# Three pairs of weight tiles moved by 32, 64 and 96 bytes in SBUF

## The chip, the cores and the metric

The kernel runs on one core of one Trainium2 chip. The metric is the device time of one execution in microseconds (us). Before the change the median of three runs is 2806.64 us (2805.08 to 2807.08).

## The reference, cut to what matters

Two small transformer stacks are run one after the other on one sequence of 256 tokens with 2048 features, all in float32. The first has two layers: a mixer (a recurrent and a gated-delta branch in the even layer, three kinds of sparse attention in the odd one) and a gated feed-forward block of inner width 5632. The second has two layers of attention variants with narrower projections. Nearly all of the arithmetic is in products of this kind:

```python
z = (u @ w_in).astype(jnp.float32)            # 256 x 2048 by 2048 x up to 8208
gate, up = jnp.split(u @ w_gu, 2, axis=-1)    # 256 x 2048 by 2048 x 11264
return (jax.nn.silu(gate) * up) @ w_down      # 256 x 5632 by 5632 x 2048
return o.astype(u.dtype) @ w_out
```

Every weight is used once per execution, and 481 MB are moved by DMA in all.

## The kernel before, in words

**The products.** A float32 matrix product is made of three products in the faster format fp32r. The activations are split into a high and a low part (`UTH`, `UTL` for the input of a stage; `HTH`, `HTL` for the hidden layer of the feed-forward block), and so are the weights (`WH`, `WL`). The kernel adds high by high, high by low and low by high. The activation tile of 128 x 128 is TensorE's stationary operand (LDWEIGHTS), and 512 columns of a weight tile are the moving operand. Lines 1105 to 1107 do this in `col` (input projections and the first feed-forward product), lines 1152 to 1154 in `row` (output projections and the second feed-forward product).

**The weights.** They come in slots of 512 KB, 1024 float32 elements on each of 128 partitions. The SP queue loads a slot into one of four `RAW` tiles. ScalarE copies it rounded to fp32r into `WH` (line 1628), VectorE writes the difference of `RAW` and `WH` to `WL` (line 2150), and TensorE then does 12 matmuls with it. A pair `WH`, `WL` is called a home. Three homes are allocated on their own (`NW = 3`) and take turns for most slots; each is used again three slots later. Six further homes (`XH`, `XL`) lie over parts of the tiles `WORK` and `BIG` and are used only for some slots at the end of each stage and the start of the next, when those parts are free.

**Two other kinds of matmul that the prediction reads.** The step `nar` (lines 1121 and 1122) handles two narrow groups of weight columns: there the weight tile in a home is the stationary operand (32 or 96 columns of it), and `UTH` or `UTL` is the moving one, with 256 columns. The step `hg_e` (lines 1354 and 1355) multiplies stationary tiles in `ZR`, which lies over `BIG`, with moving columns of the constant tile `WC`, in fp32r too.

**The order.** The order in which the steps are issued on each engine is written out ahead of time by one function (`write_order`), and every engine follows it; semaphores hold an engine back until its operands are there. The change doesn't touch this order.

**Where the tiles lie.** Tiles are allocated one behind the other. The lengths of `UTH`, `UTL` (16,384 bytes each on a partition) and of every home tile (4,096 bytes) are multiples of 256, and so is that of `WORK`. So `UTH`, `UTL`, all `WH` and `WL`, `WORK` and the start of `BIG` have one and the same remainder by 256. `HTH`, `HTL`, `XH` and `XL` are placed over `WORK` and `BIG` at multiples of 256 bytes and have it too. `BIG` is 65,664 bytes long, which is 128 more than a multiple of 256, so that `RAW`, `H`, `WC` and what follows stand 128 bytes off. The second half of `ZR` (tokens 128 to 255) begins 32,832 bytes behind its first, which puts it 64 bytes off.

Of the kernel before, what the change touches and what calls it, by code (L numbers as in the profile page):

```python
# [8 lines left out]
F32R = mybir.dt.float32r  # L9
# [7 lines left out]
SLOT = 1024  # L17
NRAW = 4
NW = 3
# [164 lines left out]
def v3(ap, a):  # L184
    return ap.rearrange("p (a b) -> p a b", a=a)
# [594 lines left out]
def build(nc, A, out):  # L780
    with ExitStack() as ctx:
        def sb(name, n, dt=F32):
            return ctx.enter_context(nc.sbuf_tensor(name, [128, n], dt))

        def over(name, n, at):

            return nc.alloc_sbuf_tensor_at(name, [128, n], dtype=F32R, offset=at)[:]
# [6 lines left out]

        UTH = sb("UTH", NKT * 256, F32R)[:].rearrange("p (k n) -> p k n", k=NKT)
        UTL = sb("UTL", NKT * 256, F32R)[:].rearrange("p (k n) -> p k n", k=NKT)
        WHL = [(sb(f"WH{i}", SLOT, F32R)[:], sb(f"WL{i}", SLOT, F32R)[:]) for i in range(NW)]
        work_at = -(-nc.sbuf_base // 32) * 32
        WORK = sb("WORK", 10752)[:]
        big_at = -(-nc.sbuf_base // 32) * 32  # L800
# [4 lines left out]
        room = [work_at + 4096 * i for i in range(8)] + [big_at + 4 * a for a in (5184, 6400, 7424, 15360)]  # L805
        WHL += [(over(f"XH{i}", SLOT, room[2 * i]), over(f"XL{i}", SLOT, room[2 * i + 1])) for i in range(NX)]
        WC = sb("WC", 9 * 128, F32R)[:]
# [190 lines left out]
        def slot_of(s):  # L998
            src, kk, wd = slots[s]
            n = kk * wd  # L1000
            wh, wl = WHL[home[s]]
            if wd < 64:
# [43 lines left out]
        def tensor(e):  # L1046
# [64 lines left out]
            def nar(st, c, k, s):  # L1111
                wd = WIDTHS[st][c]
                both = v3(WHL[home[s]][0][:, 0:16 * wd], 8)
                if k == 0:
# [1832 lines left out]
```

## Time and profile before

| what | value |
|---|---|
| median of three runs | 2806.64 us |
| the profiled execution, its own time | 2806.17 us |
| its span, first to last instruction | 2804.4 us |
| mean granted TensorE clock | 0.999 of full speed |
| TensorE (PE) busy | 2778.6 us, 99% of the span |
| VectorE (DVE) busy | 1577.9 us, 56% |
| ScalarE (ACT) busy | 1369.2 us, 49% |
| DMA | 481 MB, mean 172 GB/s |

Busy time is a union: matmuls overlap in the pipeline, so one matmul is listed with some 390 ns although the next one starts some 227 ns after it. For the rate of TensorE the distance between starts is read, not the duration. `PEld` is the loading of the stationary operand, which overlaps the matmul before it. The page is divided into 40 slices of 70 us, and PE is at 9 tenths or more in all but the last.

### The profile page before, as it was taken

Reading aid. Unit: us, or ns where it says so; the run is one execution under the profiler, and the core shown is the slowest. Engines: PE = TensorE matmul, PEld = TensorE weight load, DVE = VectorE, ACT = ScalarE, POOL = GpSimd, SP = SyncE. Lnnn points to the kernel's source line nnn. Section 1 sums busy time; section 2 is a strip of 40 time slices with the busy share of each in tenths; the row PEclk is TensorE's granted clock in tenths of the full one; section 3 lists DMA queues with packets and bytes.
Section 4 is the critical chain, followed back from the end, with each engine's and each line's share of the span. In section 5 each row is a group of like instructions: output and inputs, shape, how many; then the busy total and the mean of one; then the engine's idle time right before and its main releaser. Section 6 shows DMA issues by size and latency. Waiting matters only on the chain.

```text
span 2804.4 us, 33205 instructions
## 1 busy us (share of the span) xinstructions
PE 2778.6 (99%) x13548; PEld 2318.0 (83%) x13548; DVE 1577.9 (56%) x2212; ACT 1369.2 (49%) x2031; POOL 62.0 (2%) x83
## 2 busy tenths in 40 slices
PE   9999999999999999999999999999999999999998
PEld 8788888888888888888888888888888888887777
DVE  6665677755445454444644555654545544466666
ACT  6645454545444444333634544644444443356565
POOL 0000000000000000000010000000000000000002
PEclk9999999999999999999999999999999999999999
DMA  7855544665656555555655434566565555565444
GB/s 234 139 128 131 108 106 99 165 211 180 189 186 191 191 188 189 193 193 192 219 170 156 136 106 151 191 192 190 188 192 188 188 191 192 195 206 170 152 142 135
DMA packets 213497, 481.12 MB, mean 172 GB/s; under 512 B 15584, under 2 KB 16352, under 8 KB 212704
## 3 DMA queue, kind: packets, MB, share of 16 engines
q1 hardware_dynamic: 210848, 467.78, 55.0%
q0 software_dynamic: 2352, 11.17, 1.1%
q8 instruction: 106, 1.74, 0.3%
q14 instruction: 47, 0.39, 0.0%
q10 hardware_dynamic: 144, 0.05, 0.0%
HBM read 476.84 MB, written 2.10 MB: 171 GB/s over the span
## 4 chain that ended last, share of the span: by engine, by line
PE 90%; DVE 5%; ACT 2%; DMA 1%; issue 1%; POOL 0%; SPq 0%; ACTq 0%; POOLq 0%
PE PS L1105 19%; PE PS L1107 19%; PE PS L1106 18%; PE PS L1152 8%; PE PS L1154 8%; PE PS L1153 8%; DVE WL L2150 1%; DVE WORK L2309 1%; PE PS L1366 1%; ACT WH L1628 1%; PE PS L1269 1%; PE PS L1486 1%; PE PS L1184 1%; PE PS L1281 1%; PE PS L1282 1%
## 5 line engine op out<-in xcount | busy, mean ns | idle before, releaser
L2150 DVE TENSOR_TENSOR WL<-RAW,WH 128x1024 fp32r<-128x1024 f32 x826 | 1010.9, 1225 | 934.0 <-ACT WH L1628 932.6
L1628 ACT ACTIVATE WH<-RAW 128x1024 fp32r<-128x1024 f32 x830 | 875.1, 1055 | 833.9 <-PE PS L1107 526.3
L1105 PE MATMUL PS<-WH,UTH 128*128 128x512 f32 x2396 | 955.9, 399 | 3.4 <-DVE WL L2150 3.0
L1107 PE MATMUL PS<-WH,UTL 128*128 128x512 f32 x2396 | 935.0, 390 | 0.0
L1106 PE MATMUL PS<-WL,UTH 128*128 128x512 f32 x2396 | 933.8, 390 | 0.0
L1105 PEld LDWEIGHTS PS<-WH,UTH 128*128 128x128 f32 x2396 | 450.2, 188 | 98.8 <-issue 3.7
L1107 PEld LDWEIGHTS PS<-WH,UTL 128*128 128x128 f32 x2396 | 449.8, 188 | 97.2
L1106 PEld LDWEIGHTS PS<-WL,UTH 128*128 128x128 f32 x2396 | 450.6, 188 | 87.2
L1152 PE MATMUL PS<-WH,HTH 128*128 128x512 f32 x656 | 255.4, 389 | 0.0
L1153 PE MATMUL PS<-WL,HTH 128*128 128x512 f32 x656 | 255.2, 389 | 0.0
L1154 PE MATMUL PS<-WH,HTL 128*128 128x512 f32 x656 | 255.2, 389 | 0.0
L1153 PEld LDWEIGHTS PS<-WL,HTH 128*128 128x128 f32 x656 | 123.1, 188 | 25.7
L1152 PEld LDWEIGHTS PS<-WH,HTH 128*128 128x128 f32 x656 | 123.1, 188 | 25.4
L1154 PEld LDWEIGHTS PS<-WH,HTL 128*128 128x128 f32 x656 | 123.1, 188 | 25.4
L1152 PE MATMUL PS<-WH,UTH 128*128 128x512 f32 x256 | 102.1, 399 | 1.4 <-DVE UTL L2198 1.4
L1154 PE MATMUL PS<-WH,UTL 128*128 128x512 f32 x256 | 99.9, 390 | 0.0
L1153 PE MATMUL PS<-WL,UTH 128*128 128x512 f32 x256 | 99.7, 390 | 0.0
L2755 POOL TENSOR_TENSOR SM<-SM 128x1 f32<-128x1 f32 (+2 forms) x25 | 27.5, 1100 | 2347.6 <-DVE SM L2154 2347.6
L2150 DVE TENSOR_TENSOR XL<-RAW,XH 128x1024 fp32r<-128x1024 f32 x53 | 63.9, 1218 | 13.4 <-ACT XH L1628 13.3
L1659 ACT ACTIVATE UTH<-PS,GP 128x128 fp32r<-128x128 f32 x160 | 46.3, 387 | 40.4 <-PE PS L1080 40.4
L1628 ACT ACTIVATE XH<-RAW 128x1024 fp32r<-128x1024 f32 x53 | 55.3, 1066 | 19.4 <-DMA RAW<-in_ffn_w_down 7.8
L1752 ACT ACTIVATE HTH<-PS 128x512 fp32r<-128x512 f32 x44 | 26.1, 599 | 78.2 <-PE PS L1184 78.2
(421 smaller groups left out, 2412.5 us busy)
## 6 DMA issues: line engine op xcount, KB each, us to landing
RAW<-in_ffn_w_gu SPq DMA_DIRECT2D x352, 512.0 KB, 4.2
RAW<-in_ffn_w_down SPq DMA_DIRECT2D x176, 512.0 KB, 4.5
RAW<-in_ab_w_in SPq DMA_DIRECT2D x128, 512.0 KB, 4.7
RAW<-in_nsa_w_in SPq DMA_DIRECT2D x80, 512.0 KB, 3.6
RAW<-in_w_in SPq DMA_DIRECT2D x64, 512.0 KB, 4.0
RAW<-in_ab_w_out SPq DMA_DIRECT2D x32, 512.0 KB, 4.6
RAW<-in_nsa_w_out SPq DMA_DIRECT2D x32, 512.0 KB, 4.0
RAW<-in_w_out SPq DMA_DIRECT2D x16, 512.0 KB, 4.4
```

Source lines behind the costliest of these rows:

```text
L1105: e.matmul(o, lh, wh[:, j], start=k + j == 0, stop=False)
L1106: e.matmul(o, lh, wl[:, j], start=False, stop=False)
L1107: x = e.matmul(o, ll, wh[:, j], start=False, stop=k + j == NKT - 1)
L1152: e.matmul(o, lh, wh[:, 0, cs], start=k == (0 if hf else LEFT[st][0]), stop=False)
L1153: e.matmul(o, lh, wl[:, 0, cs], start=False, stop=False)
L1154: x = e.matmul(o, ll, wh[:, 0, cs], start=False, stop=k == (KTILES[st] - 1 if hf else LEFT[st][-1]))
L1184: x = e.transpose(b[:, 128 * j:128 * j + 128], g[:, 128 * j:128 * j + 128], ident)
L1269: x = e.matmul(b[:, 128 * h:128 * h + 128], LT[:, h], XX[:, h, 0], start=True, stop=True)
L1281: e.matmul(bb[:, 0:128], XX[:, h, 1], Y[:, h], start=True, stop=True)
L1628: e.activation(wh, raw, ACTF.Copy).then_inc(*a_hi.inc(s))
L1659: e.activation(UTH[:, kk, 128 * t:128 * t + 128], b[:, 128 * j:128 * j + 128], ACTF.Copy, scale=GP[:, st, kk:kk + 1]).then_inc(*a_ut.inc(" ...
L2150: e.tensor_tensor(wl, raw, wh.bitcast(F32), ALU.subtract).then_inc(*v_lo.inc(s))
```

## The change

Unused gaps of 8 float32 elements (32 bytes on each partition) are allocated in front of each of the three homes. They add up: the first home stands 32 bytes off its former remainder, the second 64, the third 96. A last gap of 160 bytes behind the third home brings the sum to 256, so that `WORK`, `BIG`, `RAW` and everything behind them move by 256 bytes and keep their remainders. The six homes over `WORK` and `BIG` keep theirs as well. No instruction is added, removed or reordered; only addresses differ.

```diff
-        WHL = [(sb(f"WH{i}", SLOT, F32R)[:], sb(f"WL{i}", SLOT, F32R)[:]) for i in range(NW)]
+        WHL = []
+        for i in range(NW):
+            sb(f"GAP{i}", 8)
+            WHL.append((sb(f"WH{i}", SLOT, F32R)[:], sb(f"WL{i}", SLOT, F32R)[:]))
+        sb("GAP", 40)
```

## Rows read from the trace of the kernel before

**Rows 1.** The page, part 1: busy time, share of the span and instructions of each engine.
```profile
PE 2778.6 (99%) x13548; PEld 2318.0 (83%) x13548; DVE 1577.9 (56%) x2212; ACT 1369.2 (49%) x2031; POOL 62.0 (2%) x83
```
**Rows 2.** The page, part 4: the chain that ended last, by engine, by line.
```profile
PE 90%; DVE 5%; ACT 2%; DMA 1%; issue 1%; POOL 0%; SPq 0%; ACTq 0%; POOLq 0%
PE PS L1105 19%; PE PS L1107 19%; PE PS L1106 18%; PE PS L1152 8%; PE PS L1154 8%; PE PS L1153 8%; DVE WL L2150 1%; DVE WORK L2309 1%; PE PS L1366 1%; ACT WH L1628 1%; PE PS L1269 1%; PE PS L1486 1%; PE PS L1184 1%; PE PS L1281 1%; PE PS L1282 1%
```
**Rows 3.** Waits of PE: who waited for whom, total us, times, longest us.
```profile
PE PS L1105 <- DVE WL L2150: 3.0, 6, 0.7
PE PS L1354 <- DVE ZR L2427: 1.7, 1, 1.7
```
**Rows 4.** Windows, first feed-forward block: stretch, length, busy by engine, PEclk, DMA.
```profile
620.00:1350.00 730.00, 730.00 (x3277) 603.78 (x3276) 368.75 (x360) 318.82 (x370) 2.36 (x4) 1.00 0.59 190
```
**Rows 5.** PE groups by form: count | busy us, mean ns | idle before.
```profile
L1105 PE MATMUL PS<-WH,UTH 128*128 128x512 f32 x2396 | 955.9, 399 | 3.4 <-DVE WL L2150 3.0 <-DVE WL L2167 0.2
L1152 PE MATMUL PS<-WH,HTH 128*128 128x512 f32 x656 | 255.4, 389 | 0.0
L1152 PE MATMUL PS<-WH,UTH 128*128 128x512 f32 x256 | 102.1, 399 | 1.4 <-DVE UTL L2198 1.4
```
**Rows 6.** PE timeline: start us, us, what; undisturbed stretch of the down product.
```profile
1199.69 0.39 PE L1153 MATMUL PS<-WL,HTH 128*128 128x512 f32 x1
...
1227.34 0.39 PE L1152 MATMUL PS<-WH,HTH 128*128 128x512 f32 x1
```
**Rows 7.** Line 1105: duration ns min/median/max of loads and matmuls.
```profile
L1105 PEld LDWEIGHTS PS<-WH,UTH x2396: 186/188/192, 9.4 to 2768.8; 128*128 128x128 f32 x200
L1105 PE MATMUL PS<-WH,UTH x2396: 387/389/582, 9.4 to 2769.0; 128*128 128x512 f32 x200
```
**Rows 8.** PE timeline, the narrow step: home as stationary operand.
```profile
84.33 0.28 PE L1122 MATMUL PS<-UTL,WH 128*32 128x256 f32 x1
...
87.80 0.28 PE L1122 MATMUL PS<-UTL,WH 128*32 128x256 f32 x1
```
**Rows 9.** Line 1121: duration ns min/median/max of its loads.
```profile
L1121 PEld LDWEIGHTS PS<-UTH,WH x32: 107/135/165, 84.1 to 1428.4; 128*32 128x32 f32 x16, 128*96 128x96 f32 x16
```
**Rows 10.** PE timeline: moving tile WC, then the homes, no break between.
```profile
268.55 0.50 PE L1354 MATMUL PS<-WC,ZR 128*128 128x512 f32 x1 [1.69 <-DVE ZR L2427]
268.89 0.39 PE L1355 MATMUL PS<-WC,ZR 128*128 128x512 f32 x1
...
269.58 0.40 PE L1105 MATMUL PS<-WH,UTH 128*128 128x512 f32 x1
...
272.12 0.39 PE L1107 MATMUL PS<-WH,UTL 128*128 128x512 f32 x1
```
**Rows 11.** PE timeline: the homes after four transposes.
```profile
950.49 0.60 PE L1184 MATMUL PS<-MK,BIG 128*128 128x128 f32 x4
950.84 0.48 PE L1105 MATMUL PS<-WH,UTH 128*128 128x512 f32 x1
951.16 0.40 PE L1106 MATMUL PS<-WL,UTH 128*128 128x512 f32 x1
...
953.47 0.39 PE L1107 MATMUL PS<-WH,UTL 128*128 128x512 f32 x1
953.71 0.60 PE L1184 MATMUL PS<-MK,BIG 128*128 128x128 f32 x4
```
**Rows 12.** Lines 2150 and 1628: duration ns min/median/max, by home tile.
```profile
L2150 DVE TENSOR_TENSOR WL<-RAW,WH x826: 1204/1225/1821, 12.1 to 2783.6; 128x1024 fp32r<-128x1024 f32 x166
L2150 DVE TENSOR_TENSOR XL<-RAW,XH x53: 1207/1217/1227, 610.1 to 2785.9; 128x1024 fp32r<-128x1024 f32 x53
L1628 ACT ACTIVATE WH<-RAW x830: 293/1061/1102, 11.0 to 2782.5; 128x1024 fp32r<-128x1024 f32 x165, 128x384 fp32r<-128x384 f32 x1
```

## The prediction, written before the changed kernel was run

> **What bounds the kernel now.** I read the busy times first: PE is busy for 99% of the span, DVE for 56%, ACT for 49% [rows 1]. The reader is to see that one engine fills the time. The chain of waits agrees: 90% of it is PE, and the six lines of the weight products (1105 to 1107, 1152 to 1154) hold 80% by themselves; the first DVE entry, line 2150, has 1% [rows 2]. The waits of PE come next: the largest, on line 2150's `WL`, is 3.0 us in six waits [rows 3]. So neither the preparation of weights nor their loading sets the time; what counts is how fast TensorE takes one matmul after the other. In the feed-forward block PE is busy for all of 730 us at a granted clock of 1.00, the upper level of 2.4 GHz [rows 4].
>
> The last view is the timeline, for the distance between starts. From 1199.69 to 1227.34 us there are 122 steps from one start to the next with nothing in between, so one takes 27.65 / 122 = 226.6 ns [rows 6]. 512 columns at 2.4 GHz are 213.3 ns. **The excess is 13.3 ns per matmul**, and it is the only thing on the critical path that an address could touch. How many matmuls have a moving operand in one of the three homes that move? Three kinds by (2396 + 656 + 256) = 3 x 3308 = 9924 [rows 5]. The excess over them is 9924 x 13.3 ns = 132 us. One nanosecond per matmul is 9.9 us, 0.35% of the time.
>
> **The change part by part.**
>
> *Instructions.* The gaps issue none, and order, semaphores and DMAs are as before. Cost: 0.
>
> *ACT and DVE.* They write the homes at other addresses, and DVE reads them. The bound of what an address may do to them is taken from their own spread: line 2150 has 1204 to 1225 ns (minimum, median) in the homes and 1217 ns in the six others, and line 1628 has a median of 1061 ns [rows 12]. Say 20 ns either way for each of 826 slots. That is 16.5 us of an engine that is idle for 44% of the time. On the chain line 2150 has 1%, some 28 us [rows 2]; 2% of this is 0.6 us. PE's waits for it would move by six times 20 ns [rows 3]. I take 0 and keep 1 us either way. If TensorE became faster by the whole excess, 12 matmuls per slot would take 12 x 213 = 2.56 us against 1.23 us of DVE, so there is cover in that case too.
>
> *TensorE, the moving operand.* This is the whole question, and the trace has no matmul that reads at 32, 64 or 96 bytes off. I bound it by the rows.
>
> From below: the whole excess goes, -132 us. The nearest row to a smaller gain is the spread of line 1105: the shortest matmul lasts 387 ns against a median of 389 [rows 7]. 2 ns on each of 9924 is -20 us.
>
> What the excess depends on can be read in two places. In the narrow step 30 steps from start to start take 87.80 - 84.33 = 3.47 us, 115.7 ns each [rows 8]; 256 columns at 2.4 GHz are 106.7 ns, an excess of 9.0 ns. There the load of the next stationary tile is of 32 columns (107 ns, against 188 ns for 128 columns [rows 7, 9]), and the start of that tile moves by 128 bytes from one pair to the next. So with a quarter of the loaded columns, half of the moving columns and a stationary operand that alternates between two remainders, two thirds of the excess are still there. That speaks for a cost of starting and streaming a matmul rather than for one of two reads that meet in the same place in memory.
>
> The second place is `hg_e`. Its moving tile `WC` stands 128 bytes off, its stationary tile 0. Three steps from 268.89 to 269.58 us take 0.69 us, 230 ns each [rows 10]: not below 226.6. A relative remainder of 128 brings no gain. The sample is small and lies right behind a wait.
>
> From above: after an interruption the rate isn't at 226.6 at once. From 951.16 to 953.71 us there are 11 steps in 2.55 us, 231.8 ns each [rows 11]. I call this settling; it costs 11 x 5.2 = 57 ns. The same is seen with no interruption at all where the moving tile changes from `WC` to a home: from 269.58 to 272.12 us 11 steps take 2.54 us, 230.9 ns each, 47 ns in excess [rows 10]. If each change between homes had to settle anew, 826 times 57 ns would be +47 us. It is an upper end, since slots behind an interruption pay this already.
>
> A smaller upward term: the excess grows with the columns, from 9.0 ns at 256 to 13.3 ns at 512 [rows 6, 8]. An operand that starts in the middle of a piece needs one piece more. With 16 pieces of 32 columns, one more is 13.3 / 16 = 0.8 ns: 9924 x 0.8 = +8 us.
>
> I take 0 for this part. It is the value nearest to what both places show, and the ends -132 and +47 us stay for the range.
>
> The Trainium skill ("SBUF — State Buffer", section Specifications) gives lines of 16 bytes. By that rule, 32, 64 and 96 bytes are whole lines, every read begins at a line as before, and the sum stays 0; no row shows a line. It also says ("TensorE: Matmul & The Clock Gate", section Step-by-step: what each phase is for) that the load of the next weights has its own read port and takes nothing from the running matmul. By that the stationary and the moving tile can't meet, whatever their remainders, and the change does nothing. Rows 8 agree in part. The same page ("Back-to-back issue gap") has 512 / 2.4 + 2.5 = 215.8 ns for a warm matmul of 512 columns, 10.8 ns below this kernel's; if the homes' old remainder were the reason for the difference, an estimate from that page would be 9924 x 10.8 ns = 107 us of gain. The trace has no fp32r matmul at that rate.
>
> *The sum* is 0. It is made against the profiled execution: span 2804.4 us, and 1.8 us around it, 2806.17 us. The median of the runs is 2806.64 us, 0.5 us above. I predict 2806.5 us.
>
> **The rivals.**
>
> *Faster: the two reads of TensorE meet, and the new remainders part them.* For it: the excess is there in each matmul and too regular to come from other engines, and the settling after an interruption shows that the distance depends on how the load and the matmul stand to each other, which is what two readers in each other's way would show. Against it: rows 8 and 10. Its time runs from 2806 - 20 = 2786 us (2 ns per matmul) to 2806 - 132 = 2674 us. The homes differ, so that one offset may help and another not; I take the row's 2 ns to a third of the excess (44 us) as its usual size, 2762 to 2786 us.
>
> *Slower: each change of home unsettles the stream.* Today all homes have one remainder, and going from home to home costs nothing: in the 122 steps of rows 6 there are some ten such changes. With three remainders each change moves the moving operand against the stationary one by 32 bytes or more, as the step from `WC` to the homes does. It decides at each slot's first matmul, and costs at most 47 us, 2853 us; half of it, if the next remainder is near, gives 2830 us. Against it: rows 10 are one case, itself close behind a wait of 1.69 us, and the stationary tile changes there too.
>
> *Slower by a little: one piece more per read.* 2806 + 8 = 2814 us.
>
> *The change doesn't do what it says.* The allocator could round starts up to a coarser boundary and swallow the gaps. Then the time is 2806 us as in the main case.
>
> **How the numbers follow.** The forecast of no change, the swallowed gaps included, gets 0.39; its own range is 2802 to 2811 us. The faster rival gets 0.33, of which 0.12 is for a gain over 40 us. The unsettled stream gets 0.18 and the longer read 0.10. A change of under 0.2%, 5.6 us, can't be told from none here. So faster 0.33, same 0.39, slower 0.28. The range reaches down to 2766 us, which leaves out the deep gains (0.12), and up to 2842 us, which leaves out the full settling (0.06).
>
> **What would show it.** Right: the same 122 steps in 27.6 us in the down product, a median of 389 ns on lines 1105 and 1152, and unchanged waits of PE. Faster rival: starts closer than 226 ns in the undisturbed stretches, with a step between homes. Unsettled stream: distances of 224 to 236 ns that return at every twelfth matmul. Longer read: an even 227.4 ns. If starts are as before but DVE's or ACT's durations move by over 20 ns, I was wrong on those, and the time should still stand. The prediction as a whole is wrong if the distance in those stretches moves by over 0.6 ns either way.

## The result, and the profile after

The changed kernel takes 2848.98 us (median of four runs, 2848.07 to 2850.08) against 2806.06 us for the kernel before on the same chip (2805.08 to 2807.08). The ratio is 1.0151, 95% interval 1.0138 to 1.0163: **slower by 43 us, 1.5%**. The forecast was no change, 2806.5 us, with a range up to 2842 us; it was wrong, and the range too narrow. Some runs of every kernel in the first set of experiments, the kernel before included, had a mean granted clock of 0.997 instead of 0.999 and took 5 to 8 us longer, which widens the intervals given there.

The page, parts 1 and 4, of the changed kernel. All lines below 797 have moved down by 4, so line 1105 is 1109 here.

```profile
PE 2823.1 (99%) x13548; PEld 2318.8 (81%) x13548; DVE 1578.4 (55%) x2212; ACT 1368.1 (48%) x2031; POOL 61.7 (2%) x83
...
PE 92%; DVE 4%; ACT 2%; issue 1%; DMA 1%; POOL 0%; SPq 0%; ACTq 0%; POOLq 0%
```

PE is busy for 44.5 us more than in [rows 1], with the same number of instructions, and the other engines for as long as before to within 1.1 us. PE's share of the chain grew from 90% [rows 2] to 92%. The whole loss is on TensorE. Its largest wait, 3.0 us before [rows 3], hardly changed:

```profile
PE PS L1109 <- DVE WL L2154: 2.6, 6, 0.7
```

The median durations of VectorE's and ScalarE's work on the homes (line, counts, ns minimum/median/maximum, as in [rows 12]) are within 2 ns of before:

```profile
L2154 DVE TENSOR_TENSOR WL<-RAW,WH x826: 1206/1226/1639, 12.2 to 2826.4; 128x1024 fp32r<-128x1024 f32 x166
L1632 ACT ACTIVATE WH<-RAW x830: 294/1059/1101, 11.1 to 2825.3; 128x1024 fp32r<-128x1024 f32 x165, 128x384 fp32r<-128x384 f32 x1
```

The granted clock is 1.00 in the first feed-forward block, as in [rows 4]; the columns of this window are stretch, length, busy time by engine, PEclk, DMA share and GB/s. 3250 matmuls are in 740 us, 4.39 per us, where it was 3277 in 730 us, 4.49.

```profile
630.00:1370.00 740.00, 740.00 (x3250) 599.36 (x3249) 365.56 (x354) 314.75 (x364) 1.79 (x3) 1.00 0.61 185
```

Line 1109's matmul has a median of 395 ns against 389 [rows 7]; its load is unchanged at 188 ns:

```profile
L1109 PEld LDWEIGHTS PS<-WH,UTH x2396: 185/188/193, 9.4 to 2811.5; 128*128 128x128 f32 x200
L1109 PE MATMUL PS<-WH,UTH x2396: 387/395/587, 9.4 to 2811.7; 128*128 128x512 f32 x200
```

The timeline says where. These are the first matmuls of four slots in a row in the undisturbed down product, the second feed-forward product (start us, us, what), in the same product as [rows 6]. By the written order the first of them is in the second home (64 bytes off), then come the third (96), the first (32) and the second again.

```profile
1220.17 0.40 PE L1156 MATMUL PS<-WH,HTH 128*128 128x512 f32 x1
...
1222.93 0.40 PE L1156 MATMUL PS<-WH,HTH 128*128 128x512 f32 x1
...
1225.74 0.39 PE L1156 MATMUL PS<-WH,HTH 128*128 128x512 f32 x1
...
1228.54 0.40 PE L1156 MATMUL PS<-WH,HTH 128*128 128x512 f32 x1
```

A slot is 12 matmuls. It takes 2.76 us in the home at 64 bytes, 2.81 us in the one at 96 and 2.80 us in the one at 32: 230.0, 234.2 and 233.3 ns per matmul, where before it was 226.6 in all three. **Each home has a speed of its own.** I added up the distances from each of the 10,560 large matmuls to the next one where both are of that kind: 2372.4 us before, 2417.6 us after, +45.2 us. That is the whole of the 43 us, within 2 us. In the home at 64 bytes the first distance of a slot is 237 to 241 ns and the others are 225 to 232 ns; in the home at 96 bytes they run from 231 to 240 ns to the slot's end.

### The profile page after: what moved, and what is told of

The parts are those of the page before. It is cut to its first block, busy times and chain, and to the rows that moved or that the text cites. A ratio compares the mean times of both kernels' runs of the same rounds, so it can differ in the third digit from the quotient of the medians.

```text
span 2847.1 us, 33205 instructions
## 1 busy us (share of the span) xinstructions
PE 2823.1 (99%) x13548; PEld 2318.8 (81%) x13548; DVE 1578.4 (55%) x2212; ACT 1368.1 (48%) x2031; POOL 61.7 (2%) x83
## 4 chain that ended last, share of the span: by engine, by line
PE 92%; DVE 4%; ACT 2%; issue 1%; DMA 1%; POOL 0%; SPq 0%; ACTq 0%; POOLq 0%
PE PS L1109 19%; PE PS L1110 19%; PE PS L1111 19%; PE PS L1156 8%; PE PS L1158 8%; PE PS L1157 8%; DVE WL L2154 1%; PE PS L1370 1%; DVE WORK L2313 1%; PE PS L1273 1%; PE PS L1490 1%; PE PS L1188 1%; ACT WH L1632 1%; PE PS L1285 1%; PE PS L1286 1%
## 5 line engine op out<-in xcount | busy, mean ns | idle before, releaser
L1111 PE MATMUL PS<-WH,UTL 128*128 128x512 f32 x2396 | 945.4, 395 | 0.0
L1110 PE MATMUL PS<-WL,UTH 128*128 128x512 f32 x2396 | 945.4, 395 | 0.0
L1158 PE MATMUL PS<-WH,UTL 128*128 128x512 f32 x256 | 101.1, 395 | 0.0
L1157 PE MATMUL PS<-WL,UTH 128*128 128x512 f32 x256 | 100.9, 394 | 0.0
```

Of the source, the lines that this page charges most:

```text
L1110: e.matmul(o, lh, wl[:, j], start=False, stop=False)
L1111: x = e.matmul(o, ll, wh[:, j], start=False, stop=k + j == NKT - 1)
L1157: e.matmul(o, lh, wl[:, 0, cs], start=False, stop=False)
L1158: x = e.matmul(o, ll, wh[:, 0, cs], start=False, stop=k == (KTILES[st] - 1 if hf else LEFT[st][-1]))
```

## The experiments

Unless a diff says otherwise, gaps are put so that everything but the named tiles keeps its remainder. "At 32" means 32 bytes off the old common remainder. The diffs are shortened to the lines that matter, and `k` counts the tiles of 128 rows of the weight matrix, 44 in the down product.

**all32, all64, all96: one remainder for all homes.** Two of my theories fit a sum of 43 us. Either each home's own remainder has a price, or it is the change from one remainder to the next that has one. The forecast's slower rival was the second, and its price, up to 47 us, hit the sum well.

```diff
-            sb(f"GAP{i}", 8)
+            if i == 0: sb("GAP0", 8)     # 16 in all64, 24 in all96
...
-        sb("GAP", 40)
+        sb("GAP", 56)                    # 48 in all64, 40 in all96
```

> All three homes stand 32 bytes off, with no change of remainder from home to home. Level theory (the distance between starts is set by the remainder of the moving tile against the stationary one, home by home): 233.2 ns per matmul in the undisturbed stretches, as the first home shows in the changed kernel, so 9924 x (233.2 - 226.7) = +65 us, 2871 us. Settling theory (it is the change from one home's remainder to the next that costs): 226.7 ns and about 2807 us, apart from the few changes to the six other homes.

> All three homes 64 bytes off. Level theory: 229.0 ns, the level that the second home reaches in the changed kernel, +23 us, 2829 us. Settling theory: 226.7 ns and about 2807 us.

> All three homes 96 bytes off. The third home of the changed kernel has a mean of 234.1 ns but no steady distance within its 12 matmuls. Level theory: about 234 ns, +73 us, 2879 us; if that home was still settling when it ended, its steady distance may lie lower, down to 230 ns, 2840 us. Settling theory: 226.7 ns and about 2807 us.

Measured: all32 2856.75 us, ratio 1.0168 (1.0150 to 1.0186); all64 2821.42 us, 1.0043 (1.0027 to 1.0059); all96 2858.93 us, 1.0174 (1.0157 to 1.0190). The timelines of the down product, first row and last of four slots, 48 distances; all32, then all64, then all96:

```profile
1223.49 0.40 PE L1157 MATMUL PS<-WH,HTH 128*128 128x512 f32 x1
...
1234.69 0.40 PE L1157 MATMUL PS<-WH,HTH 128*128 128x512 f32 x1
```

```profile
1208.40 0.39 PE L1157 MATMUL PS<-WH,HTH 128*128 128x512 f32 x1
...
1219.39 0.39 PE L1157 MATMUL PS<-WH,HTH 128*128 128x512 f32 x1
```

```profile
1225.20 0.39 PE L1157 MATMUL PS<-WH,HTH 128*128 128x512 f32 x1
...
1236.40 0.39 PE L1157 MATMUL PS<-WH,HTH 128*128 128x512 f32 x1
```

11.20, 10.99 and 11.20 us over 48 are 233.3, 229.0 (228.9 before the starts are rounded) and 233.3 ns, though no home differs from the next. The settling theory wanted 226.7 in all three and falls. The level theory holds. Its times were too high by 14, 8 and 20 us: I had multiplied the difference by all 9924 matmuls, but in stretches that are often interrupted the kernel before has 228.5 ns already, so there the loss is smaller (all32 has 233.1 there). For all96 the level was also 0.8 ns lower than assumed. The mean of the three times is 2845.7 us. The changed kernel has a third of each and takes 2849.0 us, so **some 3 us of the 43 are left for changing from home to home**. This difference of 3.3 us is no wider than the intervals of the runs that it is made of, some 4 us each way, and they stand on two chips. The traces show that it isn't nothing: in the down product the changed kernel's mean distance is 232.5 ns against 231.8 for the mean of the three levels, and on all matmuls in the homes those 0.65 ns would be 6 us. It is a small part either way.

**ut64: is it the tile's place or its place against the stationary one?**

```diff
+        sb("GAPU", 16)                   # UTH, UTL, WH, WL at 64
         UTH = sb("UTH", NKT * 256, F32R)[:]...
...
+        sb("GAP", 48)                    # behind the homes
```

> UTH, UTL and the three homes all stand 64 bytes off the old remainder; HTH and HTL keep it. So in the input projections and the attention output projections the moving and the stationary tile agree again, and in the down product they differ by 64 bytes. If the remainder of the moving tile against the stationary one counts: 226.7 ns in the projections, 229.0 ns in the down product, 1968 x 2.3 ns = +5 us, 2811 us. If the moving tile's own remainder counts: 229.0 ns in both, 2829 us. Settling theory: 226.7 ns in both, 2807 us.

Measured: 2812.50 us, ratio 1.0018 (1.0006 to 1.0029), the 2811 us of the first theory within its interval. The timeline, 48 distances each: the gate and up product, where both tiles stand at 64, and the down product, where only the homes do.

```profile
667.43 0.39 PE L1112 MATMUL PS<-WL,UTH 128*128 128x512 f32 x1
...
678.31 0.39 PE L1112 MATMUL PS<-WL,UTH 128*128 128x512 f32 x1
...
1203.60 0.39 PE L1158 MATMUL PS<-WH,HTH 128*128 128x512 f32 x1
...
1214.58 0.39 PE L1158 MATMUL PS<-WH,HTH 128*128 128x512 f32 x1
```

10.88 us are 226.7 ns, and 10.98 us are 228.8 ns (228.9 before rounding, the level of all64). Where the tiles were moved together nothing was lost. The six homes over `WORK` and `BIG` kept their place, so that in the projections they stand 64 bytes below `UTH` and `UTL`: their mean distance rose from 229.1 to 233.5 ns (interruptions left out) though they weren't moved. **What counts is the moving tile's remainder against the stationary one's.**

**utl32: one of the two stationary tiles.**

```diff
+        sb("GAPU", 8)
         UTL = sb("UTL", NKT * 256, F32R)[:]...
+        sb("GAP", 56)
```

> Only UTL stands 32 bytes off; UTH, HTH, HTL and all homes keep the old remainder. While the matmul of line 1105 streams WH, UTH is loaded for line 1106; while line 1106 streams WL, UTL is loaded for line 1107; while line 1107 streams WH, UTH is loaded for the next. If the moving tile meets the tile that is loaded meanwhile, one distance of three changes, after line 1106, by up to 6.7 ns and by at most 2.2 ns on average in the projections: 2596 x 6.7 = up to +17 us, 2825 us, and 226.7 ns stay in the down product. If it is the matmul's own stationary tile, the distance after line 1107 changes instead. If the moving tile's own remainder counts, nothing changes: 2807 us.

Measured: 2844.27 us, ratio 1.0135 (1.0119 to 1.0150). No theory had that. First the gate and up product, then the down product, 48 distances each:

```profile
673.50 0.40 PE L1112 MATMUL PS<-WL,UTH 128*128 128x512 f32 x1
...
684.70 0.40 PE L1112 MATMUL PS<-WL,UTH 128*128 128x512 f32 x1
...
1220.97 0.39 PE L1158 MATMUL PS<-WH,HTH 128*128 128x512 f32 x1
...
1231.85 0.39 PE L1158 MATMUL PS<-WH,HTH 128*128 128x512 f32 x1
```

The down product, which doesn't read `UTL`, stays at 226.7 ns. The other has 233.3 ns on average: the same price as if all pairs were 32 bytes apart, though only one of three is. By line:

```profile
675.36 0.40 PE L1111 MATMUL PS<-WH,UTH 128*128 128x512 f32 x1
675.60 0.40 PE L1112 MATMUL PS<-WL,UTH 128*128 128x512 f32 x1
675.84 0.39 PE L1113 MATMUL PS<-WH,UTL 128*128 128x512 f32 x1
676.06 0.40 PE L1111 MATMUL PS<-WH,UTH 128*128 128x512 f32 x1
```

On average over the gate and up products, the distance to the next start is 238.9 ns after the matmul that streams `WL`, during which `UTL` is loaded, 228.4 after the one that uses `UTL` and 232.4 after the third. The longest is where the moving tile and the tile being loaded meanwhile differ, as one theory said; but the others grew as well, so the price doesn't add up pair by pair. That a delay is carried into the next matmuls would explain it and isn't shown. It isn't shown either that the moving tile has to be one of the pair: in this run `UTL` also differs from `UTH`, the tile loaded before and after it. The loads last 188 ns as before.

**p128, p16, wlx: other remainders, and a search for a better one.** The first diff is p128's, the second p16's, the third wlx's, in which only the `WL` move.

```diff
-            sb(f"GAP{i}", 8)
+            sb(f"GAP{i}", (32, 8, 8)[i])             # at 128, 160, 192
...
-        sb("GAP", 40)
+        sb("GAP", 16)
```

```diff
+            at, n = homes_at + 8192 * i + off // 32 * 32, off % 32 // 4    # off is 16, 48, 224
+            WHL.append((over(f"WH{i}", SLOT + n, at)[:, n:], over(f"WL{i}", SLOT + n, at + 4096)[:, n:]))
```

```diff
+            at = homes_at + 8448 * i                 # off is 64, 128, 192
+            WHL.append((over(f"WH{i}", SLOT, at), over(f"WL{i}", SLOT, at + 4096 + off)))
```

> A probe of three more remainders: the homes stand 128, 160 and 192 bytes off. Relative-remainder theory: each home has a distance of its own again. The case of UTH 64 bytes above the six other homes (192 relative) had about 233 ns, so the third home should be near 233; a pattern that repeats every 128 bytes would give 226.7 ns for the first and 233 for the second, but would need 229 for the third. A pattern symmetric about 128 would give 229 for the third as well and is already in doubt. If 128 is free of it altogether, the first home has 216 to 226 ns and all homes at 128 would beat the kernel before.

> Three further remainders: 16, 48 and 224 bytes. If the levels come from a grid of 32 bytes or coarser, 16 behaves like 0 or 32 (226.7 or 233.3 ns) and 48 like 32 or 64 (233.3 or 229.0). If the start of a read inside a 32-byte unit costs a piece of its own, both lie above 233 ns. 224 tells whether a moving tile 32 bytes below the stationary one costs the same as one 32 above (233.3 ns) or not. A theory in which the remainder 0 is the best of all puts all three above 226.7.

> All WH keep the old remainder; WL stands 64, 128 and 192 bytes off in the three homes. A search for a layout better than the kernel before: one of three matmuls streams WL while UTL (or HTL) is loaded. utl32 had a distance of 233.3 ns with a single pair 32 bytes apart. If the common remainder is the best there is, all three homes have means above 226.7 ns (229 to 233). A home below 226.7 ns would be a layout to use: 1 ns is 10 us.

Measured: p128 2852.67 us, 1.0165 (1.0148 to 1.0182); p16 2846.06 us, 1.0140 (1.0125 to 1.0156); wlx, one run, 2839.66 us against 2806.08 us. A slot's length in the timeline is 12 distances of its home. In p128 this is a slot of the home at 128 bytes, its first matmul and that of the next slot:

```profile
1227.65 0.39 PE L1157 MATMUL PS<-WH,HTH 128*128 128x512 f32 x1
...
1230.43 0.39 PE L1157 MATMUL PS<-WH,HTH 128*128 128x512 f32 x1
```

2.78 us over 12 are 231.7 ns (231.6 in the mean of all such slots). All levels stand in this table; those of p128 and p16 are means of the distances in one home over the down products, which hold what is left from the home before:

| remainder, bytes | distance, ns | read from |
|---|---|---|
| 0 | 226.7 | rows 6, before rounding |
| 16 | 231.7 | p16 |
| 32 | 233.3 | all32 |
| 48 | 230.1 | p16 |
| 64 | 228.9 | all64 |
| 96 | 233.3 | all96 |
| 128 | 231.6 | p128 |
| 160 | 233.7 | p128 |
| 192 | 232.4 | p128 |
| 224 | 233.9 | p16 |

In wlx the three homes have means of 231.1, 233.2 and 230.0 ns with `WL` at 64, 128 and 192. A grid of 32 bytes is refuted (16 is neither 0 nor 32), and so is a repeat every 128. A piece of its own for a start inside a 32-byte unit asked for more than 233 ns at 16 and 48 bytes, and falls as well. 32 bytes below the stationary tile (224) cost 233.9 ns, nearly what 32 above do. Nothing is below the common remainder, and **no layout tried beats the kernel before**.

**m32at0, m32at32, m64at32: a smaller load.** If the reads of the load get in the way of the moving stream, fewer of them should cost less.

```diff
+                        m = 32 if st in (1, 3) and 0 < k < KTILES[st] - 1 else 128
-                        e.matmul(o, lh, wh[:, 0, cs], ...)
+                        e.matmul(o[0:m], lh[:, 0:m], wh[:, 0, cs], ...)    # the same for the other two
```

> Homes as before. In the down product all matmuls but the first and last k load only 32 of the 128 columns of the stationary tile, so the load lasts 107 ns instead of 188; three quarters of those output rows are left out (the output isn't the reference's). If the excess over 213.3 ns comes from the load's reads meeting the moving tile's, it shrinks with the load, to a quarter if it is proportional: 213.3 + 3.3 = 217 ns in the down product. If it belongs to the moving stream alone: 226.7 ns.

> As m32at0, with all homes 32 bytes off. If the load's reads meet the moving tile's, the 6.7 ns that 32 bytes cost shrink with the load, to some 1.7 ns: 218 to 219 ns. If the price of 32 bytes is that of a read that begins inside a piece, it stays at 6.7 ns above m32at0 whatever is loaded.

> As m32at32 with 64 columns loaded in place of 32. Load theory: between m32at32 and all32, near 213.3 + 20 / 2 = 223 ns. Moving-stream theory: 233.3 ns, as in all32.

Measured, one run each: 2815.91, 2855.49 and 2850.85 us against 2806.08 us. m32at0, 48 distances in the down product:

```profile
1134.82 0.40 PE L1154 MATMUL PS<-WL,HTH 128*32 128x512 f32 x1
...
1145.94 0.40 PE L1154 MATMUL PS<-WL,HTH 128*32 128x512 f32 x1
```

11.12 us are 231.7 ns: with a quarter of the load, 107 ns long, the distance at the common remainder *grew* by 5 ns. m32at32 has 233.3 ns (11.20 us) and m64at32 230.8 ns (11.08 us). The load theory had two halves, and they fared differently. The excess over 213.3 ns at the common remainder should have shrunk with the load; it grew, so that half is refuted. The *price of 32 bytes* should have shrunk from 6.7 ns to a quarter, 1.7 ns; it did: 11.20 - 11.12 = 0.08 us over 48 distances are 1.7 ns, where a price of the moving stream alone would have stayed at 6.7. One pair of runs can't say whether this is a proportion or a coincidence of two levels, and with 64 columns loaded the partner at the common remainder wasn't run. Fewer loaded columns are also fewer output rows, so these runs change both. That load and stream stand in each other's way by their timing fits all of this and is argued, not shown.

**n256at0, n256at32: 256 moving columns.** Each matmul of the down product is made as two; k 0 and the last are left whole.

```diff
+                        for a, z in ((0, 256), (256, 512)):
+                            cc = slice(512 * n + a, 512 * n + z)
+                            e.matmul(o[:, a:z], lh, wh[:, 0, cc], ...)    # the same for the other two
```

> Homes as before. In the down product each matmul of 512 columns is made as two of 256 for all but the first and last k. If the excess of 13.3 ns is paid per matmul (a handover): 106.7 + 13.3 = 120 ns each. If it belongs to the moving stream (a share of its columns): 106.7 + 6.7 = 113.3 ns each and no change of the time. The narrow step had 115.7 ns at 256 columns with 32 loaded.

> As n256at0 with all homes 32 bytes off. Handover theory: 106.7 + 20 = 126.7 ns each. Stream theory: 106.7 + 10 = 116.7 ns each.

Measured, one run each: 2833.27 and 2861.86 us against 2806.59 us. 96 distances of each, n256at0 first:

```profile
1131.46 0.28 PE L1156 MATMUL PS<-WH,HTH 128*128 128x256 f32 x1
...
1142.98 0.28 PE L1156 MATMUL PS<-WH,HTH 128*128 128x256 f32 x1
```

```profile
1150.17 0.28 PE L1161 MATMUL PS<-WH,HTH 128*128 128x256 f32 x1
...
1161.48 0.28 PE L1161 MATMUL PS<-WH,HTH 128*128 128x256 f32 x1
```

11.52 / 96 = 120.0 ns: at the common remainder the excess is 13.3 ns for 256 columns as for 512. This is what **a price per matmul** gives, 32 cycles of 2.4 GHz. But these runs also load 128 columns for every 256 moving ones, and the loads may set a part of the 120.0 ns. The kernel before has a case where little but the loads is left: eight float32 matmuls (not fp32r) of 15 moving columns, each with a load of 128:

```profile
1487.35 0.96 PE L1447 MATMUL PS<-WORK 128*128 128x15 f32 x8
```

From the second on they start 111 to 112 ns apart. So a floor of the loads near 112 ns is a rival for the last 8 ns, and no run here parts the two. At 32 bytes 11.31 / 96 = 117.8 ns: neither theory, and less than at 0. So 32 bytes are 6.7 ns worse at 512 columns and 2.2 ns better at 256. The kernel is slower all the same: its other products stay at 512, and two halves of 117.8 ns are longer than one whole of 226.7.

**bf16at0, bf16at32: 2 bytes per column.** For k 0 to 21 of the down product the same tiles are read as bfloat16 (the stationary view begins 2 bytes into its tile); the true sum then starts at k 22, so half of that product is left out.

```diff
+                        if st in (1, 3) and k < 22:
+                            cb = slice(1024 * n, 1024 * n + 512)
+                            lh, ll = lh.bitcast(BF)[:, 1::2], ll.bitcast(BF)[:, 1::2]
+                            e.matmul(o, lh, wh[:, 0].bitcast(BF)[:, cb], ...)    # and the other two
```

> Homes as before. In the down product the matmuls of k 0 to 21 read the same tiles as bfloat16 (512 moving columns of 2 bytes, 128 stationary columns at a step of 4 bytes); their sums are thrown away, so half of that product is left out. If the excess needs 4 bytes per moving column: 216 ns or less than 220, against 226.7 in k 22 to 43. If it doesn't: 226.7 ns.

> As bf16at0 with all homes 32 bytes off. If the sensitivity to the remainder comes from the 4 bytes per moving column, the distance in k 0 to 21 equals that of bf16at0 within 0.5 ns, against 233.3 ns in k 22 to 43. If not, 6 to 7 ns more than in bf16at0.

Measured, one run each: 2794.61 and 2838.05 us against 2806.59 us. bf16at0 first, then bf16at32; 49 distances each (of one matmul between them the record is missing):

```profile
1134.36 0.38 PE L1157 MATMUL PS<-WH,HTH 128*128 128x512 bf16 x1
...
1144.94 0.38 PE L1158 MATMUL PS<-WL,HTH 128*128 128x512 bf16 x1
```

```profile
1152.20 0.38 PE L1162 MATMUL PS<-WH,HTH 128*128 128x512 bf16 x1
...
1162.77 0.38 PE L1163 MATMUL PS<-WL,HTH 128*128 128x512 bf16 x1
```

10.58 us and 10.57 us: 215.9 and 215.7 ns, the same at both remainders. With bfloat16 32 bytes don't matter (no other remainder was tried) and four fifths of the excess are gone. Two things changed here at once, the width of the moving columns and the load, which lasts 98 ns in place of 188; the run doesn't say which of them frees it. The back-to-back distance in the Trainium skill ("TensorE: Matmul & The Clock Gate", Back-to-back issue gap), 215.8 ns at 512 columns, agrees with these rows and holds for no fp32r row here.

## Why the prediction was wrong

*The bound: right.* TensorE sets the time, the distance between starts is the quantity to read, there are 9924 matmuls concerned, and one nanosecond on each is 9.9 us. The sign named for being wrong, a distance that moves by over 0.6 ns, came: it moved by 3.4 to 7.6 ns. PE's busy time grew by 44.5 us and the time by 43.

*ACT, DVE and the waits: right.* Medians moved by 1 and 2 ns, the largest wait of PE from 3.0 to 2.6 us.

*TensorE's moving operand: the step that failed.* "I take 0 for this part" should have been +43 us, 4.3 ns on each of the 9924 matmuls on average. In the undisturbed stretch the distance went from 226.7 to 230.0, 234.2 and 233.3 ns. Two readings led to the 0.

The narrow step [rows 8] was read as evidence that the excess is a cost of starting and streaming, on which addresses have no hold. It has 256 moving columns and a short load, and n256at0, n256at32 and m32at0 show that both change how the remainder acts. A case that differs in three sizes can't stand in for the one in question. That the excess grows with the columns, from 9.0 to 13.3 ns, which priced the longer read, wasn't in these rows either: n256at0 has 13.3 ns at 256 columns with the full load.

The second reading is of `WC`, 128 bytes off, with three steps of 230 ns each [rows 10]. I wrote "not below 226.6" and concluded that a remainder of 128 brings no gain. That much is right: p128 has 231.6 ns there. But a case that shows no gain doesn't show that there is no loss, and these steps were *above* 226.6. They couldn't price the loss either. They lie behind a wait, and behind an interruption the homes at the common remainder are no faster, as the first three steps of [rows 11] show, from 951.16 to this start:

```profile
951.86 0.39 PE L1106 MATMUL PS<-WL,UTH 128*128 128x512 f32 x1
```

0.70 us, 233 ns each. So the trace before held no row for the term, and the 0 was a choice without one. The slow steps where `WC` gives way to a home [rows 10] fit a price of a differing remainder and fit the settling behind a wait; they decide nothing.

*The slower rival: right time, wrong mechanism.* "Each change of home unsettles the stream" had an upper end of 2853 us, 4 us from the result. all32, all64 and all96 have no such change among the three homes and lose 49, 14 and 51 us against the kernel before (15 runs, 2807.81 us). Its sign is there, a longer first distance at each twelfth matmul in the home at 64 bytes, but of the rival's 47 us only some 3 to 6 us are real. Had only the sum been compared, this story would have stood: that its time came close was luck.

*The rule of separate ports.* That the load takes nothing from the running matmul, as the Trainium skill has it ("TensorE: Matmul & The Clock Gate", Step-by-step: what each phase is for), was given as a reason for no change. For fp32r the rows differ: utl32 moves only `UTL`, which is loaded everywhere but in 32 matmuls of the narrow step, and costs 38 us. The measurement decides.

*The faster rival* assumed that a common remainder is the bad case. It is the best of the ten measured at 512 columns. *Longer read:* 227.4 ns everywhere was expected, from pieces of 32 columns that no row shows; the levels are 229 to 234. *Swallowed gaps:* they act.

*The range* ended at 2842 us because I gave the full unsettling 0.06. An unmeasured sensitivity on a quantity where 1 ns is 10 us deserved a wider top.

**What stays open.** Why the levels are what they are. Shown: with fp32r they depend on the moving tile's remainder against the tiles loaded, and what it costs depends on how many columns are loaded and how many move. Not shown: whether in bfloat16 the narrower columns or the shorter load take the dependence away, and whether the 13.3 ns at 256 columns are those at 512. That two streams of reads meet in the same parts of the memory fits the rest; it is argued, not shown. Of its simple forms, a sum pair by pair is refuted and so is an excess that shrinks with the load, while the price of 32 bytes did shrink with it, in the one case tried.

## What to carry to other kernels

Where TensorE is busy all the time with fp32r products, take the distance between starts in an undisturbed stretch, and treat a change of SBUF addresses as a possible change of speed: here 32 bytes cost 3% per matmul. Keep the moving and the stationary tiles at one remainder by 256 unless a measurement of the very shape says otherwise; an added or resized tile in front of them can shift it unseen, and the instruction counts will show nothing. When a rival's number fits, still run the experiment in which its mechanism can't act.

## What the runs showed of the hardware

- At one remainder, an fp32r matmul with a load of 128 columns has an excess of 13.3 ns over its columns both at 512 (226.7 ns) and at 256 (120.0 ns). In bfloat16, with a load of 98 ns in place of 188, it is 2.5 ns at 512 columns (215.8), at 0 and at 32 bytes.
- Remainders from 16 to 224 bytes give 228.9 to 233.9 ns at 512 columns; at 256 columns 32 bytes give 117.8 ns, less than 0 does.
- A shorter load isn't cheaper at 512 columns: 32 columns in place of 128 raised the distance from 226.7 to 231.7 ns. At 32 bytes both have 233.3 ns, so the price of 32 bytes fell from 6.7 to 1.7 ns.
- A single stationary tile of two at another remainder, 32 bytes off, costs as much as both (233.3 ns), though the durations of the loads stay at 188 ns.
- Loads of 128 float32 columns with hardly any moving columns (15) between them start 111 to 112 ns apart, though each lasts 187 to 192 ns.
